# Moving side work of the delta rule to GpSimd, overlapping the second substitution, and reordering grams in a two-block transformer kernel

## The reference, cut to what matters

```
decay = exp(where(incl, g[..., :, None] - g[..., None, :], -inf))
kb = k * beta[..., None]
lower = where(strict, einsum('bhncd,bhnsd->bhncs', kb, k) * decay, 0.0)
rhs = concatenate([v * beta[..., None], kb * exp(g)[..., None]], axis=-1)
sol = triangular_solve(eye(C) + lower, rhs, unit_diagonal=True)
u, wk = split(sol)
intra = where(incl, einsum('bhncd,bhnsd->bhncs', q, k) * decay, 0.0)
# per chunk: v_new = u - wk @ S;  o = (q * exp(g)) @ S + intra @ v_new
#            S = S * exp(g_last) + (k * exp(g_last - g))^T @ v_new
```

## Time and profile before

| what | value |
|---|---|
| median of 3 runs | 3515.9 us (3514.63 to 3524.79) |
| the profiled execution's own time | 3516.75 us |
| its span in the profile | 3514.9 us |
| mean granted clock of PE | 0.981 |
| first layer's recurrences, from the decay rows to the last output | about 616 to 769.5 us |
| the second layer's | about 1787 to 1941 us |

### The profile page before, as it was taken

One profiled execution on the slowest core, in us unless ns is written; L12 is line 12 of the kernel. 1 busy time (PEld: TensorE's weight loads), 2 busy tenths in 40 slices (PEclk: granted clock), 3 DMA queues, 4 the chain that ended last, 5 costly groups with the idle time before them and its releaser, 6 DMA issues.

```text
span 3514.9 us, 47288 instructions
## 1 busy us (share of the span) xinstructions
PE 3377.4 (96%) x16952; PEld 2779.3 (79%) x16952; DVE 1430.3 (41%) x2753; ACT 1254.3 (36%) x1892; POOL 1674.2 (48%) x2052
## 2 busy tenths in 40 slices
PE   7999998799999999999969999999899999999999
PEld 6888776688888888887658888878667888888887
DVE  5431597845221422148786522224563110341100
ACT  4222436424222322234553432233533332433321
POOL 6765552005665566655300366644304555435554
PEclk9999999899999999999989999999999999999999
DMA  5443321003443344333100244332102222212222
GB/s 184 143 144 112 106 94 60 2 7 132 143 143 114 125 143 144 123 104 96 61 25 2 87 146 144 131 103 84 66 1 84 95 95 96 78 61 102 98 99 96
DMA packets 104224, 340.50 MB, mean 97 GB/s; under 512 B 12144, under 2 KB 17936, under 8 KB 103968
## 3 DMA queue, kind: packets, MB, share of 16 engines
q1 hardware_dynamic: 87824, 283.08, 24.2%
q10 hardware_dynamic: 16272, 55.65, 4.8%
HBM read 330.78 MB, written 2.65 MB: 95 GB/s over the span
## 4 chain that ended last, share of the span: by engine, by line
issue 38%; POOL 33%; PE 27%; DVE 1%; POOLq 0%; ACT 0%; DMA 0%; SPq 0%; DVEq 0%
POOL w_lo L695 33%; PE ps L2233 7%; PE ps L2231 7%; PE ps L2232 7%; PE ps L3003 1%; PE ps L2982 1%; PE ps L2254 0%; PE ps L2991 0%; PE ps L2255 0%; PE ps L2259 0%; PE ps L3093 0%; DVE stat L2132 0%; DVE sq L2125 0%; PE ps L3099 0%; PE ps L2983 0%
## 5 line engine op out<-in xcount | busy, mean ns | idle before, releaser
L695 POOL TENSOR_TENSOR w_lo<-w_raw,w_hi 128x256 fp32r<-128x256 f32 x2040 | 1667.5, 849 | 1823.2 <-ACT w_hi L738 1817.0
L2231 PE MATMUL ps<-h_hi,w_hi 128*128 128x512 f32 x2608 | 1020.7, 391 | 0.9 <-ACT mem L955 0.9
L2233 PE MATMUL ps<-h_hi,w_lo 128*128 128x512 f32 x2608 | 1016.3, 390 | 0.0
L2232 PE MATMUL ps<-h_lo,w_hi 128*128 128x512 f32 x2608 | 1015.9, 390 | 0.0
L738 ACT ACTIVATE w_hi<-w_raw 128x1024 fp32r<-128x1024 f32 x510 | 538.5, 1058 | 916.8 <-DMA w_raw<-in_tiles 916.5
L2231 PEld LDWEIGHTS ps<-h_hi,w_hi 128*128 128x128 f32 x2608 | 490.0, 188 | 112.8 <-issue 6.1
L2233 PEld LDWEIGHTS ps<-h_hi,w_lo 128*128 128x128 f32 x2608 | 490.0, 188 | 102.6
L2232 PEld LDWEIGHTS ps<-h_lo,w_hi 128*128 128x128 f32 x2608 | 490.2, 188 | 100.6
L2232 PE MATMUL ps<-a_lo,w_hi 128*128 (+1 forms) x1120 | 437.2, 390 | 0.0
L2231 PE MATMUL ps<-a_hi,w_hi 128*128 (+1 forms) x1056 | 411.0, 389 | 0.0
L2233 PE MATMUL ps<-a_hi,w_lo 128*128 (+1 forms) x1056 | 411.0, 389 | 0.0
(11 more groups left out here) (470 smaller groups left out, 3616.9 us busy)
## 6 DMA issues: line engine op xcount, KB each, us to landing
w_raw<-in_tiles SPq DMA_DIRECT2D x510, 512.0 KB, 3.3
ada_raw<-in_ada_tiles ACTq DMA_DIRECT2D x96, 512.0 KB, 3.3
mem<-mem SPq DMA_DIRECT2D x80, 64.0 KB, 2.1
x<-in_x_t SPq DMA_DIRECT2D x2, 1024.0 KB, 6.5
sq<-in_cond ACTq DMA_DIRECT2D x4, 512.0 KB, 4.0
mem<-gates SPq DMA_DIRECT2D x8, 256.0 KB, 3.8
consts<-in_consts SPq DMA_DIRECT2D x1, 1280.0 KB, 12.7
core_mem<-gates SPq DMA_DIRECT2D x8, 128.0 KB, 2.9
```

The lines of the kernel that those rows point to most:

```text
L695: ins = nc.gpsimd.tensor_tensor(w_lo[:, s, part], w_raw[:, s, part], w_hi[:, s, part].bitcast(F32), ALU.subtract)
L2231: nc.tensor.matmul(bank, wh, hi, start=first, stop=False, skip_group_check=True)
L2232: nc.tensor.matmul(bank, wh, lo, start=False, stop=False, skip_group_check=True)
L2233: return nc.tensor.matmul(bank, wl, hi, start=False, stop=last, skip_group_check=True)
```

## The change

A function `delta_parts` on POOL, placed once per layer behind the low part of the output projection's first four tiles, takes over: the decay units of chunks 1 to 3 (two instructions of 128x512 each), k times its decay, v times beta, the corners of all four chunks, the scaling of q, and q and k times the exponential of the gates. ACT copies the spread norms of q out of PSUM for it, DVE squares q and k in ACT's place, and q's and k's norms move from the attention's loop behind it. In step 0 DVE runs chunk 1's substitution before and between the first merges of chunk 0, instead of after them; `small_blocks` works on 16 columns instead of 32. In steps 0 and 3 PE issues some of the grams of the next step. The diff, cut to what the text speaks of:

```diff
+        LAST_BANKS = (1, 7)
+        def a_unit(n, g):
+            return g if n == TB and g < 2 else C_A + g
+        def a_bank(n, g):
+            return LAST_BANKS[g % 2] if n == TB else (0, 1, 6, 7)[g]
...
@@ gpsimd
+            def delta_parts(l):
+                pool.wait_ge(S["g_taken"], l + 1)
+                pool.wait_ge(S["dt_spread"], 64 * (l + 1))
+                for n in range(1, TB):
...
+                    nc.gpsimd.tensor_tensor(heads(mem[:, 20 + n, :]), heads(mem[:, 20 + n, :]), over_heads(const("decay_neg")), ALU.add).then_inc(S["gdn_parts"], 1)
+                    pool.wait_ge(S["gdn_parts"], 10 * l + 2 * n - 1)
+                    nc.gpsimd.tensor_tensor(decay, decay, g, ALU.add).then_inc(S["gdn_parts"], 1)
+                pool.wait_ge(S["spread_taken"], 3 * l + 3)
+                pool.wait_ge(S["eg_ready"], 4 * l + 2)
+                nc.gpsimd.tensor_tensor(mem[:, 24:26, :], mem[:, U_KG:U_KG + 2, :], mem[:, U_DELTA:U_DELTA + 2, :], ALU.mult).then_inc(S["gdn_parts"], 1)
+                pool.wait_ge(S["conv_act_v"], 3 * l + 3)
+                nc.gpsimd.tensor_tensor(mem[:, 37:39, :], mem[:, 37:39, :], core_mem[:, R_SQ:R_SQ + 2, :], ALU.mult).then_inc(S["gdn_parts"], 1)
+                lower_corners(l, 0)
+                pool.wait_ge(S["turned_out"], 11 * l + 1)
...
+                nc.gpsimd.tensor_tensor(q, q, sil[:, :, :], ALU.mult).then_inc(S["gdn_parts"], 1)
+                pool.wait_ge(S["turned"], 11 * (l + 1))
+                pool.wait_ge(S["gdn_parts"], 10 * l + 9)
...
+                nc.gpsimd.tensor_tensor(qe, q, eg, ALU.mult)
+                nc.gpsimd.tensor_scalar(kbe, mem[:, 39:41, :], -1.0, None, ALU.mult).then_inc(S["gdn_parts"], 1)
+                pool.wait_ge(S["gdn_parts"], 10 * l + 10)
+                nc.gpsimd.tensor_tensor(kbe, kbe, eg, ALU.mult).then_inc(S["gdn_ready"], 1)
+                for n in range(1, TB):
+                    lower_corners(l, n)
+            def lower_corners(l, n):
+                b = TB * l + n
+                pool.wait_ge(S["gram_taken"], 2 * b + 2)
+                if n == 0:
+                    pool.wait_ge(S["gdn_parts"], 10 * l + 8)
+                else:
+                    pool.wait_ge(S["dx_ready"], merge_turn(b - 1, 4, 1) + 1)
+                nc.gpsimd.tensor_tensor(all_heads(core_mem[:, C_N:C_N + 2, :]), all_heads(lower_units(n)), const("levels").unsqueeze(1).to_broadcast([P, 8, P]), ALU.mult).then_inc(S["corners_ready"], 1)
...
@@ scalar, recurrences
+                nc.scalar.activation(mem[:, U_QG:U_QG + 2, :], core_mem[:, G_CONV:G_CONV + 2, :], ACT.Silu).then_inc(S["conv_act_v"], 1)
+                load_sqrt()
+                head_roots(2, 2, 1.0, EPS_NORM, 2)
+                factors_out()
                 head_roots(3, 2, 1.0, EPS_NORM)
                 act.wait_ge(S["spread_taken"], 3 * l + 2)
-                nc.scalar.activation(mem[:, 20:24, :], mem[:, 20:24, :], ACT.Exp).then_inc(S["dt_ready"], 1)
+                nc.scalar.activation(mem[:, 20, :], mem[:, 20, :], ACT.Exp).then_inc(S["eg_ready"], 1)
+                act.wait_ge(S["gdn_parts"], 10 * l + 6)
+                nc.scalar.activation(mem[:, 21:24, :], mem[:, 21:24, :], ACT.Exp).then_inc(S["eg_ready"], 1)
...
+                act.wait_ge(S["turned"], due("turned"))
+                nc.scalar.activation(sil[:, :, :], ps[:, 2:4, :], ACT.Copy, scale=HD ** -0.5).then_inc(S["turned_out"], 1)
...
@@ vector, recurrences (before: L1795)
+                for x, (at, unit) in enumerate(((2, k), (0, q))):
+                    dve.wait_ge(S["conv_act_v"], 3 * l + x + 1)
+                    V.tensor_tensor(mem[:, U_NORMED + at:U_NORMED + at + 2, :], unit, unit, ALU.mult).then_inc(S["head_sq"], 1)
...
-                V.tensor_tensor(mem[:, 24:26, :], k, mem[:, U_DELTA:U_DELTA + 2, :], ALU.mult).then_inc(S["kd_ready"], 1)
-                V.tensor_tensor(mem[:, 37:39, :], mem[:, 37:39, :], beta, ALU.mult).then_inc(S["head_done"], 1)
-                V.scalar_tensor_tensor(q, q, HD ** -0.5, ps[:, 2:4, :], ALU.mult, ALU.mult).then_inc(S["head_done"], 1)
                 substitute(range(15, 0, -1))
-                lower_corners(0)
                 spread_inverses(l, 0)
@@ vector, small_blocks (before: L1839)
-                    ins = V.tensor_tensor(C_M32[rows], all_heads(lower_units(n)[rows])[:, :, rows], BLOCK16[rows].unsqueeze(1).to_broadcast([32, 8, 32]), ALU.mult)
+                    ins = V.scalar_tensor_tensor(C_M16[rows], blocks[:, :, 16:32], HALF32[rows, 1:2], blocks[:, :, 0:16], ALU.mult, ALU.add)
@@ vector, core_step (before: L1881)
+                if n == 0:
+                    dve.wait_ge(S["eg_ready"], 4 * l + 4)
                 if n + 1 < TB:
                     take_grams(l, n + 1)
                     small_blocks(l, n + 1)
                 if n == 0:
-                    V.tensor_tensor(mem[:, 37:39, :], mem[:, U_QG:U_QG + 2, :], mem[:, 41:43, :], ALU.mult)
-                    V.scalar_tensor_tensor(mem[:, 24:26, :], mem[:, 39:41, :], -1.0, mem[:, 41:43, :], ALU.mult, ALU.mult).then_inc(S["gdn_ready"], 1)
+                    substitute(range(15, 9, -1))
+                    merge16(0)
+                    substitute(range(9, 8, -1))
+                    merge16(1)
+                    substitute(range(8, 0, -1))
+                if 0 < n < TB:
+                    a_grams(n, (2, 3, 0, 1) if n == 1 else range(4))
                 if n == TB:
+                    a_grams(n, (2, 3))
...
+                if n + 1 < TB:
+                    if n == 0:
+                        dve.wait_ge(S["gdn_ready"], l + 1)
                     spread_inverses(l, n + 1)
+                if n == TB - 1:
+                    a_grams(TB, (0, 1))
                 if 0 < n < TB:
                     next_state()
@@ tensor, core_step (before: L2652)
                 def writes():
+                    if n == TB - 1:
+                        grams(LAST_BANKS, "a_gram_ready", ((kt, ap), (kt, rt)), n)
+                    if n == TB:
+                        grams(LAST_BANKS, "a_gram_ready", ((nb, rt), (kg, qg)), last)
...
+                if n == 0:
+                    pe.wait_ge(S["gdn_parts"], 10 * l + 9)
+                    grams((6, 7), "a_gram_ready", ((nb, rt), (kg, qg)), 0)
```

More of the change, by code:

```diff
@@ L711, in _ @@
+            cosines = BASE["dft_time"]
+            done = 0
+            for l in range(DEPTH):
+                ahead = BASE[f"mix_out{l}"] + RING
+                low_parts(done, ahead)
+                delta_parts(l)
+                done = ahead
+            low_parts(done, cosines + 2)
             pool.wait_ge(S["w_used"], BASE["dft_group"])
@@ L1042, in meanwhile @@
                         act.wait_ge(S["conv_ready"], l + 1)
[L1043 to L1047, removed]
+                        nc.scalar.activation(mem[:, U_KG:U_KG + 2, :], core_mem[:, G_CONV + 2:G_CONV + 4, :], ACT.Silu).then_inc(S["conv_act_v"], 1)
                 due("proj_out", REC_TILES)
@@ L1750, in attention @@
                 dve.wait_ge(S["g_taken"], l + 1)
[L1751 to L1755, removed]
+                for h in range(4):
+                    block = mem[:, 20, blk(2 * (h % 2) + h // 2)]
+                    ins = V.scalar_tensor_tensor(block, block, stat[:, ST_GNEG + h:ST_GNEG + h + 1], const("decay_neg"), ALU.add, ALU.add)
                 ins.then_inc(S["spread_taken"], 1)
@@ L1876, in spread_inverses @@
                 spread = lambda units: units.rearrange("p u (h q c) -> p (u h) q c", h=4, q=4)
-                quarter = QUARTER.unsqueeze(1).unsqueeze(3).to_broadcast([P, 8, 4, 32])
-                V.tensor_tensor(spread(inv_units(n)), C_X32.unsqueeze(2).to_broadcast([P, 8, 4, 32]), quarter, ALU.mult).then_inc(S["small_ready"], 1)
+                quarter = QUARTER.unsqueeze(1).unsqueeze(3).to_broadcast([P, 4, 4, 32])
+                for g in range(2):
+                    V.tensor_tensor(spread(inv_units(n)[:, g:g + 1, :]), C_X32[:, 4 * g:4 * g + 4, :].unsqueeze(2).to_broadcast([P, 4, 4, 32]), quarter, ALU.mult).then_inc(S["small_ready"], 1)
+                if n + 1 < TB:
+                    fresh_rows()
             def core_step(l, n):
@@ L2519, in meanwhile @@
                             nc.tensor.matmul(ps[:, 1, 0:P], const("ident"), const("ones"), start=True, stop=True)
-                        for at, bank in ((2, 2), (0, 3)):
-                            pe.wait_ge(S["head_sq"], due("head_sq"))
-                            head_sums(mem_units(U_NORMED + at, U_NORMED + at + 1), bank, at).then_inc(S["head_sum"], 1)
-                        for _ in range(5):
-                            nc.tensor.matmul(ps[:, 1, 0:P], const("ident"), const("ones"), start=True, stop=True)
-                        pe.wait_ge(S["head_inv"], due("head_inv"))
-                        for c in range(2):
-                            head_spread(mem[:, U_NORMED + 2 + c, :], c).then_inc(S["head_spread"], 1)
                     if i == 16:
@@ L2608, in recurrences @@
```

(6 more changed lines are left out.)

107 lines of the change are left out of this document (57 added, 50 removed).

## The result

The changed kernel takes 3525.7 us (median of 19 runs, 3520.0 to 3529.2), the kernel before 3515.0 (19 runs, 3509.5 to 3524.8): ratio 1.0027, 95% interval 1.0020 to 1.0034. That is slower beyond the noise of the runs, and by so little that it still counts as no change: the ratio lies just inside 0.3%, while its interval reaches just past it. The profiled execution's span is 3526.4 us. So I compare stretches.

The account below looks back on a forecast made before the run. PE sets the pace nearly everywhere, DVE in each layer's recurrences before step 3. Per layer -19.1 + 16.4 + 4.1 = +1.4 us, for two layers +2.8: 3519 us, no change that can be told; range 3476 to 3534.

Parts of the forecast that it names:

- exclusion by POOL: Recurrences: DVE's two-SBUF-input instructions and POOL's exclude each other; 16.4 us before the first inverse, 4.1 in steps 0 to 2.
- Start and first inverse: Each layer's start until chunk 0's inverse: 7.0 us faster without POOL's effects, 16.4 us lost to POOL.
- the piecewise reading: DVE beside POOL: a long POOL instruction lets DVE in between pieces; total 3511 us.
- Step 0: First recurrence step, 23.7 us before: 5.2 us off DVE's chain, against 1.3 to 1.4 for POOL's corner mask.
- Step 1: Second recurrence step: 2.4 us off through corners and a shorter wait for grams, against 1.3 to 1.4 for POOL's corner.
- Step 2: Third recurrence step: 1.2 us off for the corners, against 1.3 to 1.4 for POOL's corner.
- The corner's price: Steps 0 to 2: one POOL corner mask of 1024 elements stops DVE for 1.3 to 1.4 us each, 4.1 together.
- Steps 3 and 4: Last recurrence steps: step 3 1.1 us slower with grams added, step 4 4.4 us faster as right sides wait less.
- A: Recurrences: POOL works beside DVE, so the whole 19.1 us per layer shows; 3478 us, chance 0.17.
- B: Recurrences: POOL gives way inside a long instruction, 4.2 to 7.3 us less per layer; 3504 to 3511 us, chance 0.20.
- C: Small_blocks and first substitution: long POOL instructions exclude longer, 2.8 us per 1024, +9.2 us per layer; 3534 us, chance 0.20.

Follow-up runs that it names:

- e1: The changed kernel with each of POOL's new instructions cut from 512 or 1024 elements to 8, order and waits kept: 3485.6 us.
- e3: The kernel before with only the last chunk's grams moved into its step's own gaps: 3502.6 us.
- e5: e3 with filler, products of two constants on PE behind the substitution steps of chunks 0 and 1: 3500.6 us.
- e6: e3 with small blocks on 16 columns and two groups of first-chunk grams ahead in step 0, start as before: 3501.7 us.
- e4: The changed kernel with POOL's work back on DVE and both first merges of chunk 0 ahead of the second substitution: 3506.8 us.
- e2: The changed kernel with both first merges of chunk 0 ahead of the whole second substitution: 3521.3 us.
- e9: e2 with filler products on PE behind the steps of the substitutions: 3515.1 us.
- e10: e7 with fourteen more filler products per layer, in the two waits left in step 0: 3494.9 us.
- e7: e6 with filler products of constants on PE behind the substitution steps: 3491.9 us.
- e8: The changed kernel with filler products on PE behind the substitution steps of chunks 0 and 1: 3531.6 us.

## Why the prediction was right and wrong

The time came inside the range and inside "same", 6.7 us above the figure. The main mechanism, exclusion by POOL, was right and well sized; that the total came out near is partly luck, as one large miss in step 0 was more than half made up by smaller ones the other way. Per layer (first layer, predicted / measured):

- **Start and first inverse**: +9.4 / 35.4 to 43.9 = +8.5. Both halves are borne out: without POOL -7.0 / -6.2 (e1), of exclusion 16.4 / 14.7. POOL's instructions took 1.05 and 2.35 us undisturbed (estimates 1.1 and 2.2), and DVE was stopped until a two-input one was done; the one-input one cost it about 0.85 us (taken as 1.1), not its whole 2.78. The first inverse was forecast near 660; it came at 664.1, with the decay rows themselves 4.2 late. On this the Trainium skill's rule ("SBUF — State Buffer", "Who interferes with whom") stood against the piecewise reading, and the trace agrees with it for POOL's two-input instructions; the one-input one did not block DVE for its whole length.
- **Step 0**: -5.2 + 1.4 = -3.8 / +4.0. **This is the step that failed.** I took off what left DVE's chain and let that set the step. DVE's chain did shorten (its inverse of chunk 1 is written 21.4 us after level 4, at 685.4; 23.6 before), but I took the waits for the merges off as gains (0.96 and 0.3) and never walked PE's chain behind them. The merge now waits for DVE, not DVE for the merge; PE idles, runs at half clock and ends last, 6.3 us behind DVE. In e1 the predicted length appears (18.9; 23.7 - 5.2 = 18.5) in the layer where the clock was high, and in that layer alone.
- **Step 1**: -2.4 + 1.3 = -1.1 / -2.5. **Step 2**: +0.2 / -0.2. Most of the gain in step 1 is luck. I had DVE set the pace up to step 3, though the earlier trace rows have PE busy for 25.80 of 26.00 us in step 1 and for 24.98 of 26.50 in step 2. Step 1 became shorter because PE's clock was 1.00 in it, where it was 0.91 before: filler alone takes 2.2 us off it (e3 28.8, e5 26.6), and the parts that I counted, at a clock of 0.92, leave it at 28.2 (e6). The corner's price hides where PE sets the step: e1 saves 0.9 and 0.0 us there, not 1.3 and 1.4.
- **Steps 3 and 4**: +1.1 - 4.4 = -3.3 / -5.6. The mechanism was right (e3), the size of one term off: step 3 is 1.2 longer, step 4 is 6.8 shorter. PE's work in step 4 took 12.19 us at a clock of 0.78 before and takes 8.07 at 1.00 after; less the 1.16 us of grams that moved to step 3, the clock gave some 3.0 us, where I had taken 0.8.

The sum was +1.4 and is +4.2 (first layer) and +4.6 (second): step 0's 7.8 us missed, less 2.3, 1.4, 0.9 and 0.4 elsewhere. That leaves about 2 of the 10.7 us outside the recurrences, less than these medians can tell.

**The rivals.** A (POOL beside DVE for nothing) would have come near e1, 3485.6 us; the rows of DVE refute it. B (POOL gives way inside an instruction) falls with the 2.02 and 2.35 us of single DVE instructions. C needed 2.5 us per 1024 elements; it was 2.35.

**The change in parts**, along a chain of kernels from before over e3, e6, e4 and e2 to after (medians): last grams -12.6, small blocks and grams ahead -0.9 (not told from nothing), the start's new order +5.1, the work on POOL +14.6, the split substitution +4.3 (+1.4 by the ratios, not told from nothing). The parts add up to the whole because each kernel is compared with the next; that is no check of any of them. I had counted the start's order among the gains, as shorter waits: e4 shows it is a loss as soon as DVE's decay rows stand ahead of the squares. What e4's order would be worth with ACT squaring as before was not tried, nor was POOL's work in short pieces.

## What to carry over

An idle engine is no free place for another's side work if they lock each other out: POOL's 2.35 us in place of DVE's 1.2 cost DVE 2.35, and the whole list cost the kernel 14.6 us. When work is moved into a wait, ask who waited and walk the other engine's chain too: here the wait changed sides, and PE came late and at half clock. And where a change bundles several edits, run each alone: one small edit was worth 12.6 us, hidden behind two that lost.

## What the hardware showed beyond that

- The same stretch of one program was granted quite different clocks in its two layers: in e5, with PE's instructions ahead of it alike to 0.1 us over the 20 us before, step 0 ran at 0.93 and at 0.54, 23.0 and 29.0 us. A single profile of such a stretch is one draw. On this the Trainium skill ("TensorE: Matmul & The Clock Gate", part 1) says that the gate watches activity on a free-running schedule that does not start with the kernel; that fits, and no run here shows the schedule itself.
- Filler products held the clock at 1.00 through step 0 where PE's waits in it were all under 1 us (e9, e10). Behind waits of 2.1 and then 1.4 us (e7) and of 5.0 us (e8) PE fell to half clock, and behind one of 2.7 us (e5) it did so in one layer and hardly in the other. Where PE comes last, the filler itself costs time (2.50 us in e8).
- A copy with a single SBUF input (128x1024, 0.69 us alone) was held by POOL too: 2.79 us. A mask with one input in PSUM was not (0.41 us with POOL busy). A one-input product on POOL (L745, 2.78 us) let DVE's two-input instructions through 1.1 us after it began, in both layers.
